# Sixteen row groups for two query groups, and the row buffers of an expert phase handed out by age

## The reference

```
def peer_ffn(hn, wq, subkeys, u_tab, v_tab):
    q = (xt @ wq).reshape(T, 8, 2, 128)
    s = jnp.einsum('thpd,hpkd->thpk', q, subkeys)          # 128 keys for each of 8 heads x 2 halves
    s1, i1 = lax.top_k(s[:, :, 0], 16)
    s2, i2 = lax.top_k(s[:, :, 1], 16)
    cand = s1[..., :, None] + s2[..., None, :]             # 256 pairs
    top_s, pos = lax.top_k(cand, 16)
    idx = take(cand_idx, pos); gate = softmax(top_s)       # 16 experts for each of 8 heads
    act = gelu(einsum('td,thkd->thk', x, u_tab[idx]))      # dot product with the row's first half
    out = einsum('thk,thkd->td', gate * act, v_tab[idx])   # weighted sum of the second halves
```

## Time and profile before

| | us |
|---|---|
| median of 3 runs | 3253.53 (3250.49 to 3256.86) |
| the profiled execution's own time | 3253.32 |
| its span | 3251.5 |
| TensorE busy / VectorE busy | 2661.7 (82%) / 2164.0 (67%) |
| GpSimd's gathers (queue q0), share of 16 DMA engines over the span | 39.5%, 536.90 MB |

### The profile page before, as it was taken

The page is one execution under the profiler, slowest core; times in us unless marked ns, Lnnn a source line. Parts: engine busy times, 40 slices in busy tenths (PEclk is TensorE's granted clock), DMA queues, the critical chain, the costliest instruction groups (busy, mean ns, idle before and its releaser), DMA issues. The chain is left out here.

```text
span 3251.5 us, 36582 instructions
## 1 busy us (share of the span) xinstructions
PE 2661.7 (82%) x13360; PEld 1924.1 (59%) x13360; DVE 2164.0 (67%) x4130; ACT 1103.7 (34%) x1946; POOL 598.7 (18%) x547
## 2 busy tenths in 40 slices
PE   8988999998999899799776667667989786666666
PEld 7857987886898788597632222225878642222222
DVE  6366655547664574554798888865663778888875
ACT  4354443436443464344321111113644411111111
POOL 0000000000000000000344444440000245444441
PEclk9999999999999989899988888889999988888888
DMA  6423544450454333143699999996423589999996
GB/s 251 162 79 104 185 170 152 175 194 14 146 194 169 147 115 106 60 174 141 231 391 426 427 426 427 427 427 278 148 102 136 226 319 426 426 427 427 426 427 287
DMA packets 112356, 810.87 MB, mean 249 GB/s; under 512 B 12720, under 2 KB 12720, under 8 KB 14000
## 3 DMA queue, kind: packets, MB, share of 16 engines
q0 software_dynamic: 73728, 536.90, 39.5%
q1 hardware_dynamic: 38448, 271.63, 23.2%
HBM read 807.44 MB, written 1.05 MB: 249 GB/s over the span
## 5 line engine op out<-in xcount | busy, mean ns | idle before, releaser
L160 DVE TENSOR_TENSOR ring_low<-ring,parts 128x2048 fp32r<-128x2048 f32 x234 | 533.4, 2291 | 361.7 <-ACT parts L153 358.8
L3013 PE MATMUL ps<-ring,arena 128*128 128x512 f32 x768 | 430.1, 710 | 212.8 <-ACT arena L2944 212.6
L3013 PE MATMUL ps<-arena 128*128 128x512 f32 x768 | 440.1, 730 | 196.5 <-ACT arena L2944 191.4
L418 PE MATMUL ps<-parts,parts 128*128 128x256 f32 x2528 | 569.5, 283 | 8.5 <-DVE ring_low L160 5.1
L153 ACT ACTIVATE parts<-ring 128x2048 fp32r<-128x2048 f32 x234 | 444.4, 1912 | 320.8 <-PE ps L426 121.7
L418 PE MATMUL ps<-parts,ring_low 128*128 128x256 f32 x1824 | 512.3, 281 | 0.0
L426 PE MATMUL ps<-parts,parts 128*128 128x512 f32 x1344 | 447.5, 403 | 23.2 <-DVE ring_low L160 14.5
L3013 PEld LDWEIGHTS ps<-arena 128*128 128x128 f32 x768 | 172.6, 234 | 461.7 <-ACT arena L2944 264.7
L3013 PEld LDWEIGHTS ps<-ring,arena 128*128 128x128 f32 x768 | 163.1, 224 | 468.1 <-ACT arena L2944 295.2
L418 PEld LDWEIGHTS ps<-parts,parts 128*128 128x128 f32 x2528 | 428.3, 189 | 10.7 <-issue 5.3
L2855 DVE CUSTOM_DVE_ANT_0 arena<-arena 128x1024 f32<-128x1024 f32 x256 | 311.0, 1228 | 128.0 <-DMA arena<-in_experts,stage_index 126.3
(11 more groups left out here) (461 smaller groups left out, 3139.6 us busy)
## 6 DMA issues: line engine op xcount, KB each, us to landing
ring<-in_stream SPq DMA_DIRECT2D x249, 1024.0 KB, 4.8
arena<-in_experts,stage_index POOLq DMA_INDIRECT x256
ring<-in_experts,stage_index POOLq DMA_INDIRECT x256, 26.9
gain_row<-in_gain_rows SPq DMA_DIRECT2D x4, 512.0 KB, 5.7
arena<-in_mem SPq DMA_DIRECT2D x2, 1024.0 KB, 6.8
arena<-in_stream SPq DMA_DIRECT2D x2, 1024.0 KB, 7.8
par<-in_params SPq DMA_DIRECT2D x4, 386.0 KB, 3.1
x<-in_x SPq DMA_DIRECT2D x1, 1024.0 KB, 4.9
```

The source lines that it names most:

```text
L160: dve.tensor_tensor(k.ring_low[v % SLOTS], whole, self.high[:, c % self.HIGH_SLOTS, :].bitcast(F32), ALU.subtract).then_inc(self.ph.sem("c ...
L418: last = pe.matmul(self.ps[:, 2 * pair + f // 2, (f % 2) * T:(f % 2 + 1) * T], w[:, f * P:(f + 1) * P], x[:, k, :], start=(k == 0 and i == ...
L3013: last = pe.matmul(k.ps[:, bank + n, :], diag[:, s % ROWS, :], rows[row_of[s]][:, D + n * BLK:D + (n + 1) * BLK], start=(s % SLOTS_PER_TOK ...
```

## The change

It does four things. `queries(2)` and `queries(3)` are cut over row groups 2 to 17 instead of 0 to 7: the same eight pieces of 24 matmuls, one behind every second group. What hangs on them moves too: the low and high splits of their weights, the copies, the scores. The routing parts within a unit of eight groups move up by one group. The row buffers are handed out by age (`pairs_in_turn`): the pair that was used longest ago among those that are open, pair 4 opening at group 13, pair 5 at 21, pairs 6 and 7 at 22.

```diff
-ROUTE_IN_8 = {1: [0], 2: [1, 2], 3: [3], 4: [4], 5: [5], 6: [6, 7]}
-LOW_AT = {0: 4, 2: 5, 4: 6, 6: 7}
+ROUTE_IN_8 = {0: [0], 1: [1, 2], 2: [3], 3: [4], 4: [5], 5: [6, 7]}
+LOW_AT = {1: 4, 5: 5, 9: 6, 13: 7}
+PAIR_FROM = [0, 0, 0, 0, 13, 21, 22, 22]
+
+
+def pairs_in_turn():
+
+    used, order = [-8, -7, -6, -5, -12, -11, -10, -9], []
+    for g in range(GROUPS):
+        pair = min((p for p in range(8) if PAIR_FROM[p] <= g), key=lambda p: used[p])
+        used[pair] = g
+        order.append(pair)
+    return order
+
+
+PAIRS = pairs_in_turn()
...
 def pair_of(g):
 
-    return g % 4 if g < 10 else (4, 5, 6, 7, 2, 3, 0, 1)[(g - 10) % 8]
+    return PAIRS[g]
...
                 for g in range(GROUPS):
-                    if g == 3:
+                    if g == 8:
                         split.chunk_high(act, first + 7)
-                    if g == 5:
+                    if g == 10:
                         queries(2)
-                    if g == 7:
+                    if g == 12:
                         scores(2)
-                    if g == 9:
+                    if g == 18:
                         queries(3)
-                    if g == 11:
+                    if g == 20:
                         scores(3)
...
                     add_rows(g)
-                    if g < 8:
-                        queries(2 + g // 4, ks=range(2 * (g % 4), 2 * (g % 4) + 2))
-                    if g == 5:
+                    if 2 <= g < 18 and g % 2 == 0:
+                        queries(2 + (g - 2) // 8, ks=range((g - 2) % 8, (g - 2) % 8 + 2))
+                    if g == 10:
                         scores(2)
-                    if g == 9:
+                    if g == 18:
                         scores(3)
```

## The result

The changed kernel takes 3260.14 us (median of 16 runs, 3255.00 to 3268.44), the kernel before beside it 3255.23 (16 runs). The ratio is 1.0019, interval 1.0011 to 1.0026: slower by about 5 us by the medians and 6 by the ratio, around the 0.2% that the prediction takes as the border of no change. The prediction was 3248, with 3239 to 3258 as its range; the measured time lies above it. The profiled execution of the changed kernel, 3255.0 us with a span of 3253.2, is the fastest of its 16, so its trace holds only 1.7 us of the difference.

What follows compares the result with a forecast made beforehand. Behind its start-up each expert phase was taken as DMA-bound, so only filling the queue earlier helps. Layer 0 +0.3, layer 1 -3.7 and barrier -1.8 summed to -5.2 us: 3248 us, range 3239 to 3258.

Steps and rivals of the forecast that it cites:

- Groups 4, 6 and 8: Layer 0 start-up: group 4's gathers issued 2 us later, group 6's 10 us and group 8's 6.5 us earlier.
- Group 12 gives the gain back: Layer 0: group 12 waits for group 8's weights, the queue runs dry for 11 us, lead left 2.1 us.
- the block: VectorE's low split, keys and pairs in one piece, 10.5 us, ahead of group 9's dot products and group 8's weights.
- From group 12 on: Layer 0: gather 32 1.0 us earlier if groups 13 to 21 go out in time; with a slip charged, +0.3.
- one slip: Allowance of 1.3 us per layer for a late issue among groups 13 to 21, where few pairs leave little margin.
- second rival: Thin buffers: with four or five pairs until group 21, delays are lost for good; 3256 and more, chance 0.12.
- The marker: Landing of gather 32, first of group 16: what it saves the layer saves, if the queue then stays full.
- Layer 1: The same chain 1000.24 us later puts gather 32 at 2671.7 with the slip, against 2675.40: -3.7 us.
- The barrier: End of layer 0: SyncE's loads go out about 2227, so the next phase does not wait for them: -1.8 us.
- The rule on the clock: Rule against the change: idle stretches between matmul bursts halve TensorE's clock; two rows cost 5.18 us instead of 3.70.
- third rival: Queue not filled earlier, group 2's weights held by something missed: 3254; chance 0.48 together with the forecast itself.
- slow case: Late thin buffers: 11 minus some margin of 3, so 8 us lost per layer, 3264 with both layers.

Runs made afterwards that it cites:

- e1: The changed kernel with the routing parts back in their old groups, each one group later; 3247.2 us, ratio 0.9965.
- e3: The changed kernel with routing parts one by one in groups 0 to 6 and the third low split at group 7, not 9; 3245.2 us, ratio 0.9957.
- e13: The changed kernel with 28 filler matmuls on constants ahead of group 8's rows, to keep TensorE warm; 3255.2 us, ratio 1.0001.
- e5: The kernel before with only the routing parts moved up by one group; 3245.0 us, ratio 0.9973.
- e9: The changed kernel with query pieces one per group in groups 2 to 9, splits ahead of them, fifth pair from group 10, all eight from 15; 3235.3 us, ratio 0.9945.
- e16: e9 with the fifth pair opening at group 13 in place of 10; 3240.8 us, ratio 0.9956.
- e14: The changed kernel with one of three passes of the last query group's product; 3257.5 us, ratio 1.0007.
- e17: e9 with no pair after the fifth opening before groups 21 and 22; 3236.5 us, ratio 0.9952.
- e4: The kernel before with only the new order of row pairs; 3257.5 us, ratio 1.0008.
- e15: The changed kernel with the last three pairs opening at groups 27 and 28 in place of 21 and 22; 3260.6 us, ratio 1.0021.
- e6: The changed kernel with the last query group's four pieces in groups 10 to 13 and the last three pairs opened at 19 and 20; 3261.5 us, ratio 1.0024.
- e7: e3 and e6 together, on the changed kernel; 3239.1 us, ratio 0.9957.
- e2: The changed kernel with the three pairs of groups 21 and 22 opened at 23 and 24, so group 21 reuses a pair; 3260.7 us, ratio 1.0016.

## Why the prediction was wrong, step by step

*Groups 4, 6 and 8: right.* Forecast 1588.2, 1594.3 and 1611.8; measured 1587.67, 1594.21 and 1612.22. In layer 1 the forecast moved by 1000.24 gives 2588.4, 2594.5 and 2612.0; measured 2588.17, 2595.10 and 2612.57.

*Group 12 gives the gain back: right.* Forecast for group 8's weights 1636.5, measured 1636.29; group 12 at 1643.9, measured 1642.66 (the rows took 5.15 and not 6.34), in layer 1 2644.97 for 2644.1. Gather 24 landed at 1648.0, even 1.4 us before its forecast. e1 and e3 show that the block is the cause, e13 that the clock adds to it. What I had not seen is that this is a matter of pairs. The block sits in front of group 8's weights, and it matters because group 12 reuses group 8's pair. e5 has the block and not that reuse, and gains 8.6 us. e9 and e16 differ only in when the fifth pair opens, and gather 24 in 10.6 and 11.1 us. That is far more than the 3 us by which alike kernels differ.

*From group 12 on: this step failed.* The prediction said that groups 13 to 21 would go out in time, with "1.3 us for one slip". Group 14 was right (1653.4, measured 1653.47), group 16 was 1.3 us late (1664.2, measured 1665.45), group 21 4.7 us (1688.1, measured 1692.84). In layer 1 they were 2.9, 4.3 and 7.8 us late. Against before, the term of 1.3 measured 5.2 and 6.2 us: 3.7 and 3.9 at gathers 28 to 34, and 1.5 and 2.2 at gathers 40 to 46. Behind gather 46 layer 0 wins 1.1 back and layer 1 loses 0.2, which leaves the 4.1 and 6.4 of the table.

The mechanism was named, as the second rival with a chance of 0.12, but the margins were taken from TensorE at full clock. A pair's round trip, from issue to the next issue into it, was 1642.66 to 1668.60 for groups 12 and 17, 25.9 us, and 1646.03 to 1672.93 for groups 13 and 18, 26.9 us, where five pairs allow 5 x 4.92 = 24.6. But these two cost nothing yet: group 17 goes out right behind group 16 (0.30 us), and from gather 34 to 40 nothing is lost. The first loss lies at groups 14 to 16, which take the pairs of groups 9, 10 and 11. Their rows stand behind the late rows of group 8, and group 11's also behind group 10's piece and the scores: they start at 1662.70, and group 16 goes out at 1665.45, 8.2 us behind group 15, where a group lands in 4.92. The second loss is group 21, which waits for the end of `queries(3)`. Group 16's rows stand ahead of the last piece. They came late, as gather 35, which the forecast's pace puts at 1677.6, landed at 1681.1. Then, behind 3.17 us of idling, they took 5.40 us, 1.7 more than at full clock. The last piece came behind them, and the release behind that.

What the experiments show of the causes: the pieces' time on TensorE is a part of the first loss (e14, 1.7 and 2.1 us less). Few pairs are a part of it even without pieces, while the queue is still catching up (from gather 28 to 34 e17 loses 2.7 and 1.9 us against e9, e4 2.2 in layer 0 and nothing in layer 1; e16, with eight pairs there, loses nothing), and not in a full queue behind it (e15, e17). The second loss goes away when the query product ends earlier (e4, e6, e7, e17) and stays when group 21 only takes another pair (e2, e15); in e1 it is missing in layer 1, unexplained. Opening the last pairs at 19, 23 or 27 instead of 21 moves the time by 1.4 us at most. How the first loss divides between pieces, pairs and clock stays open.

The marker was part of the failure. What it saves was to be what the layer saves, "as long as the queue then stays full". From the first landing to gather 32 the changed kernel is 0.5 and 0.9 us ahead of before. From gather 32 to 46 it then loses 3.7 and 3.1, with the DMA share at 0.96 from 1650 to 1700 us where it had been 1.01. A marker has to lie behind the last wait that the change touches, here behind group 21.

*Layer 1: forecast -3.7, measured +2.3 at its last gather; the same step failed.* Up to group 12 it went as forecast, to 0.9 us, and group 8's rows took the 6.36 us that were charged (6.34). The slips of 2.9, 4.3 and 7.8 us come behind that. Gather 32 was waited for until 2675.02 for a forecast of 2671.7; before it was 2675.40. Four microseconds more start-up in the kernel before were no gain in hand for this one: its own layer 1 also took longer than its layer 0, by 3.2 us up to gather 24.

*The barrier: right.* The idle time before the next phase fell from 2.19 to 0.42 us, the 1.8 of the forecast. The loads went out at 2230.12; 2227 was forecast, since the last gather itself was 3 us late.

*The rule on the clock.* The rows show it: 12.37 us idle, then 5.15 and 6.36 us for rows that take 3.70 in e13. The Trainium skill, "TensorE: Matmul & The Clock Gate", section "Why this matters for your kernels", says that idle stretches between bursts cost half the clock; the trace agrees for these pauses. After 2.23 us of idling the rows paid nothing. Since I had taken dear prices for groups 4 and 8 already, the forecast failed on the rows behind them, where I had not (group 16, 5.40 us). The prediction calls this rule its third rival, but the third rival is about group 2's weights; the clock stands in the second, where its price in the slow case, 8 us a layer, came out as 5 to 6.

Where the forecast -5.2 went, by the profiled runs: layer 0 +2.1 at its last gather in place of +0.3, layer 1 +2.3 in place of -3.7. The first gather lands 0.9 us later, from the last landing of layer 0 to the first of layer 1 it is 2.5 us less (the barrier's 1.8 in it), and behind the last landing 1.2 less; but for the barrier, no step spoke of these. Together that is the 1.7 of the two spans. The medians show 3 us more than this pair of traces, and where they lie is not shown.

## What to carry to other kernels

When buffers are reused, write down for each early transfer which earlier piece of work frees its buffer, and look at what stands in front of that work on every engine. The same routing move was worth -8.6 us in one kernel and +13 in the other by the medians, where its work stood in front of weights that the next free buffer waited for. Compare round trip (issue to release) with buffers times the transfer time. A margin of 1 us in 25 is next to none, because any piece of work laid between, or a matmul at half clock, is in the round trip. And a landing that is to stand for the whole phase has to lie behind the last place where the change makes anything wait.
